# Outputs out of the partner's buffer, a ring of four row tiles, three pairs of weight buffers, slot 4 loaded behind the last store

## The reference

```
g_sel = argmax(x1 @ w_group + b_group)               # 1 of 4 groups
top_i = top_k(e_sel + e_bias, 2)                     # 2 of its 8 experts
for e in range(32):                                  # d_expert = 256
    gu = xt @ w_gate_up[e]                           # 1024 x 512
    h = silu(gu[:, :256]) * gu[:, 256:]
    y = y + gate[:, e:e+1] * (h @ w_down[e])         # 256 x 1024
out = layernorm(ALPHA * x1 + y, ln2_g, ln2_b)
```

## Time and profile before

| | us |
|---|---|
| median of 3 runs | 601.82 (601.57 to 604.54) |
| the profiled execution | 602.56 |
| its span | 600.9 |
| PE busy | 518.8 (86%) |
| DVE busy | 373.2 (62%) |
| ACT busy | 191.4 (32%) |
| POOL busy | 134.0 (22%) |
| chain that ended last | PE 56%, DMA 26%, DVE 8%, ACT 7% |
| queue of SP (weights) | 127.46 MB, 52.9% of the 16 engines' span |
| queue of POOL (rows) | 29.59 MB, 13.0% |

### The profile page before, as it was taken

How to read it: one execution, slowest core, us unless ns; L and a number is a source line. 1 busy time by engine, 2 the same in 40 slices (tenths; PEclk the granted TensorE clock), 3 DMA queues, 4 the chain that set the end, 5 groups by cost and what they waited for, 6 DMA issues and landing times.

```text
span 600.9 us, 8960 instructions
## 1 busy us (share of the span) xinstructions
PE 518.8 (86%) x3296; PEld 281.0 (47%) x3296; DVE 373.2 (62%) x722; ACT 191.4 (32%) x356; POOL 134.0 (22%) x156
## 2 busy tenths in 40 slices
PE   5999999999979879899999898888887777767761
PEld 4887788874355443445556743333332222222220
DVE  1642059898933576652258666677886477666686
ACT  0100374214243644121142122444444244432340
POOL 1001054500025760000000201233323222221231
PEclk9999999999979999999999899999999899999997
DMA  9940008570606932001978599999999999999951
GB/s 302 405 155 6 1 1 331 213 269 1 279 5 230 395 116 87 2 1 59 417 290 342 180 420 406 409 396 419 415 415 411 419 418 419 415 415 418 401 193 43
DMA packets 34010, 157.95 MB, mean 263 GB/s; under 512 B 12680, under 2 KB 12680, under 8 KB 20016
## 3 DMA queue, kind: packets, MB, share of 16 engines
q1 hardware_dynamic: 20592, 127.46, 52.9%
q0 software_dynamic: 10752, 29.59, 13.0%
q10 hardware_dynamic: 2624, 0.34, 0.4%
HBM read 160.12 MB, written 21.23 MB: 302 GB/s over the span
## 4 chain that ended last, share of the span: by engine, by line
PE 56%; DMA 26%; DVE 8%; ACT 7%; issue 3%; SPq 0%; POOL 0%; DVEq 0%; POOLq 0%; ACTq 0%
DMA arena_o<-in_w_gu 19%; PE ps L489 17%; PE ps L748 8%; PE ps L962 8%; PE ps L985 4%; PE ps L651 3%; PE ps L589 2%; PE ps L635 2%; DVE arena_s L1477 2%; PE ps L672 2%; DMA first_rows<-arena_s,known 1%; DMA x_rows<-arena_s 1%; PE ps L555 1%; DMA known<-slot_table 1%; DMA slot_table<-arena_s 1%
## 5 line engine op out<-in xcount | busy, mean ns | idle before, releaser
L962 PE MATMUL ps<-arena_w,arena_s 128*64 128x512 f32 x368 | 109.2, 605 | 24.1 <-DMA arena_w<-in_w_gu 12.3
L489 PE MATMUL ps<-arena_w 128*128 128x260 f32 x416 | 94.5, 388 | 6.7 <-DMA arena_w<-in_w_in 6.2
L489 PEld LDWEIGHTS ps<-arena_w 128*128 128x128 f32 x416 | 79.7, 193 | 21.0 <-DMA arena_w<-in_w_in 6.2
L962 PEld LDWEIGHTS ps<-arena_w,arena_s 128*64 128x64 f32 x368 | 33.2, 139 | 96.9 <-issue 66.4
L985 PE MATMUL ps<-arena_w,cs 128*64 128x512 f32 x184 | 56.1, 615 | 20.8 <-ACT cs L1260 20.8
L748 PE MATMUL ps<-arena_o,arena_s 128*128 128x512 f32 x128 | 58.3, 601 | 1.6 <-DVE arena_s L1601 1.6
L962 PE MATMUL ps<-arena_o,arena_s 128*64 128x512 f32 x112 | 50.2, 595 | 0.0
L1477 DVE STREAM_TRANSPOSE arena_s<-arena_w 128x1024 f32<-128x1024 f32 x36 | 41.8, 1214 | 8.3 <-PE ps L589 8.2
L2150 POOL DMA_INDIRECT first_rows<-arena_s,known x15 | 18.0, 1202 | 113.9 <-ACT arena_s L1267 105.1
L1910 DVE TENSOR_TENSOR arena_s<-arena_s,ps 128x256 f32<-128x256 f32 x16 | 6.7, 421 | 56.5 <-ACT arena_s L1256 56.5
L985 PEld LDWEIGHTS ps<-arena_w,cs 128*64 128x64 f32 x184 | 16.0, 141 | 51.0 <-issue 30.3
(11 more groups left out here) (349 smaller groups left out, 897.3 us busy)
## 6 DMA issues: line engine op xcount, KB each, us to landing
arena_w<-in_w_gu SPq DMA_DIRECT2D x46, 1024.0 KB, 19.9
arena_w<-in_w_dn SPq DMA_DIRECT2D x23, 1024.0 KB, 19.9
arena_o<-in_w_gu SPq DMA_DIRECT2D x14, 1024.0 KB, 23.2
arena_o<-in_w_dn SPq DMA_DIRECT2D x7, 1024.0 KB, 23.8
arena_w<-in_w_in SPq DMA_DIRECT2D x13, 512.0 KB, 14.1
arena_o<-in_w_out SPq DMA_DIRECT2D x1, 4096.0 KB, 13.5
arena_s<-in_w_gu SPq DMA_DIRECT2D x4, 1024.0 KB, 8.1
arena_w<-in_xT SPq DMA_DIRECT2D x4, 520.0 KB, 6.7
```

Of the source, the lines that this page charges most:

```text
L489: last = mm(ps[rows, b + n, 0:HALF], lhs(k), rhs(k)[:, n * HALF:(n + 1) * HALF], start=(k == 0), stop=(k == ks - 1))
L962: last = mm(ps[64 * e:64 * e + 64, 2 + q, :], xgT[:, k, CAP * e:CAP * (e + 1)], gu_w[2 * slots + e][:, k, :], start=(k == 0), stop=(k == K ...
```

## The change

1. **Slot 4.** Its two w_gate_up loads are issued right behind the last store of x1, ahead of the waits for the stores and for the first gather. Its w_down load stays where it was.
2. **Weight buffers.** All three pairs of buffers are used all the way, by the table `BUFFER`: pairs 3 to 15 use buffers 0, 1, 2, 0, 1, 0, 1, 2, 0, 1, 2, 0, 1. The refill for pair n waits for the pair that used its buffer last: 3 for 0, 4 for 1, 5 for 2, 6 for 3, 7 for 4, 8 for 6, 9 for 7, 10 for 5, 11 for 8, 12 for 9, 13 for 10, 14 for 11, 15 for 12.
3. **Rows.** The row tiles are a ring of four. The last operation of `finish(n)` writes the finished row into `yo[n % 2]`, the buffer that held the partner's rows, and the output leaves from there; there are two such buffers. `finish(n-1)` stands in DVE's step n, `root(n-1)` in ACT's. On POOL, step n is now `gather_other(n)` (which also waits for the landing of output n-2), `scatter_own(n)`, `scatter_out(n-1)` (behind the landing of output n-2) and `gather_rows(n+3)`; step 0 is `scatter_own(0)` alone.
4. **Residual.** `lng` is multiplied by ALPHA once, ahead of `residual(0)`. The two operations of `residual` take a minimum and a maximum with large constants in place of the multiplications by ALPHA.
5. **End.** DVE's end is `finish(14)`, `hidden(15)`, `finish(15)`; in the last, the partner's rows are added first and the own part, straight from PSUM, behind them. PE has five 128 x 128 products whose result is not used behind the last gate and up products.
6. `bounds_check` of the row DMAs is a register instead of a constant.

```diff
...
+BUFFER = (0, 1, 2, 0, 1, 0, 1, 2)
+ROW_MAX = 1e6
...
-S_XG = [5120, 6144, 0, D, S_RT] + [S_SLOT + D * n for n in range(3)]
-S_YO = [S_SLOT + 3 * D, 2 * D, S_SLOT + 4 * D]
+S_XG = [5120, 6144, 0, D]
+S_YO = [S_RT, 2 * D]
...
+def pair_buffer(n):
+    return n if n < HEAD else BUFFER[(n - HEAD) % BODY]
+def before_in(n):
+    d = 1
+    while BUFFER[(n - HEAD - d) % BODY] != pair_buffer(n):
+        d += 1
+    return d
...
         def ring(n):
-            return n % BODY
-        def other(it, n):
-            return 2 if isinstance(it, tuple) and n == NPAIR - 1 else n % 2
+            return n % 4
...
             store_x1(4)
+            for half in range(2):
+                gate_up(4, slice(4, 5), half)
             landed(sp, x1_stored, TT)
             landed(sp, gathered[0])
-            for half in range(2):
-                gate_up(4, slice(4, 5), half)
             down(4, slice(4, 5))
             sp.dma_start(lng, lns[0:2].partition_broadcast(P)).then_inc(ln1_landed, 16)
             sp.dma_start(lng2, lns[2:4].partition_broadcast(P)).then_inc(ln1_landed, 16)
-            def refill(q, e, used):
+            def refill(it, n):
+                q, used = pair_buffer(n), nth(it, n, add=1 - before_in(n))
...
                 for half, done in enumerate((gu_half, gu_ps)):
                     sp.wait_ge(done, used)
...
-            refill(0, 6, 1)
-            refill(1, 8, 2)
+                for j in range(2):
+                    down(2 * q + j, slice(e + j, e + j + 1) if isinstance(e, int) else bass.ds(e + j, 1))
+            refill(None, HEAD)
+            refill(None, HEAD + 1)
...
-            with sp.Fori(0, n_rounds * (NE // 4) - 3) as it:
-                refill(0, (it * 4 + 10) % NE, it * 2 + 4)
-                refill(1, (it * 4 + 12) % NE, it * 2 + 5)
-            refill(0, NE - 2, past + (NPAIR - 2))
+            with sp.Fori(0, n_rounds * 2 - 1) as it:
+                for n in range(HEAD + 2, HEAD + 2 + BODY):
+                    refill(it, n)
+            for n in range(HEAD + 2 + BODY, NPAIR):
+                refill((past,), n)
...
                 if not last_pair:
                     turn_tokens(it, n + 1)
+                else:
+                    for _ in range(5):
+                        mm(ps[:, 7, 0:P], ident[:, :], ident[:, :], start=True, stop=True)
...
                     own_out(it, n)
-                    root(it, n - 2)
+                    root(it, n - 1)
...
-            root((past,), NPAIR - 3)
+            root((past,), NPAIR - 2)
             hidden((past,), NPAIR - 1, True)
-            root((past,), NPAIR - 2)
             root((past,), NPAIR - 1)
...
             def residual(it, n):
                 x = xg[ring(n)]
-                stt(x, x, ALPHA, lng[:, 0, :], ALU.mult, ALU.mult).then_inc(residual_step, 1)
+                stt(x, x, ROW_MAX, lng[:, 0, :], ALU.min, ALU.mult).then_inc(residual_step, 1)
                 dve.wait_ge(residual_step, nth(it, n, 1, 2, 1))
-                stt(x, lng[:, 1, :], ALPHA, x, ALU.mult, ALU.add).then_inc(residual_step, 1)
-            def own_part(it, n, last_pair=False):
+                stt(x, x, -ROW_MAX * ROW_MAX, lng[:, 1, :], ALU.max, ALU.add).then_inc(residual_step, 1)
+            def own_part(it, n):
                 x, g = xg[ring(n)], known[:, n // QUAD % 2, 2, n % QUAD:n % QUAD + 1]
                 dve.wait_ge(known_landed, nth(it, n, QUAD, 16, 16))
                 dve.wait_ge(residual_step, nth(it, n, 1, 2, 2))
+                dve.wait_ge(ya_done, nth(it, n, add=1))
+                stt(x, yb[n % 2], g, x, ALU.mult, ALU.add).then_inc(own_added, 1)
+            def finish(it, n, last_pair=False):
+                x = xg[ring(n)]
                 if last_pair:
-                    dve.wait_ge(dn_ps, nth(it, n, add=1))
-                    y = ps[:, 5:7, :]
-                    x = x.rearrange("p (a b) -> p a b", a=2)
+                    dve.wait_ge(residual_step, nth(it, n, 1, 2, 2))
                 else:
-                    dve.wait_ge(ya_done, nth(it, n, add=1))
-                    y = yb[n % 2]
-                stt(x, y, g, x, ALU.mult, ALU.add).then_inc(own_added, 1)
-            def finish(it, n):
-                x = xg[ring(n)]
-                dve.wait_ge(own_added, nth(it, n, add=1))
+                    dve.wait_ge(own_added, nth(it, n, add=1))
                 if n > 0:
-                    dve.wait_ge(yo_landed[other(it, n)], 16 if other(it, n) == 2 else nth(it, n + 1, 2, 16))
-                    stt(x, yo[other(it, n)], known[:, n // QUAD % 2, 3, n % QUAD:n % QUAD + 1], x, ALU.mult, ALU.add).then_inc(finish_step, 1)
+                    dve.wait_ge(yo_landed[n % 2], nth(it, n + 1, 2, 16))
+                    stt(x, yo[n % 2], known[:, n // QUAD % 2, 3, n % QUAD:n % QUAD + 1], x, ALU.mult, ALU.add).then_inc(finish_step, 1)
                     dve.wait_ge(finish_step, nth(it, n, 1, 4, 1))
                     dve.wait_ge(mean_done, nth(it, n))
+                if last_pair:
+                    halves = x.rearrange("p (a b) -> p a b", a=2)
+                    dve.wait_ge(dn_ps, nth(it, n, add=1))
+                    stt(halves, ps[:, 5:7, :], known[:, n // QUAD % 2, 2, n % QUAD:n % QUAD + 1], halves, ALU.mult, ALU.add).then_inc(own_added, 1)
+                    dve.wait_ge(own_added, nth(it, n, add=1))
...
-                stt(x, x, stat[:, 2:3], lng2[:, 1, :], ALU.mult, ALU.add).then_inc(out_ready, 1)
+                stt(yo[n % 2], x, stat[:, 2:3], lng2[:, 1, :], ALU.mult, ALU.add).then_inc(out_ready, 1)
...
-                if n >= 2:
-                    finish(it, n - 2)
+                if n >= 1:
+                    finish(it, n - 1)
                 own_part(it, n)
...
+            link(ts(lng[:, :, :], lng[:, :, :], ALPHA, None, ALU.mult))
...
-            finish((past,), NPAIR - 3)
+            finish((past,), NPAIR - 2)
             hidden((past,), NPAIR - 1)
-            finish((past,), NPAIR - 2)
-            own_part((past,), NPAIR - 1, True)
-            finish((past,), NPAIR - 1)
+            finish((past,), NPAIR - 1, True)
...
             def gather_other(it, n):
...
+                if n >= 2:
+                    pool.wait_ge(out_landed, gone)
                 pool.wait_ge(scattered[(n - 1) % 2], before)
-                G.indirect_dma_start(out=yo[other(it, n)], out_offset=None, in_=first_rows,
+                G.indirect_dma_start(out=yo[n % 2], out_offset=None, in_=first_rows,
                                      in_offset=bass.IndirectOffsetOnAxis(ap=place(1, n), axis=0),
-                                     bounds_check=TOK - 1, oob_is_err=False).then_inc(yo_landed[other(it, n)], 16)
-            def scatter_out(it, n):
-                ready, = number(nth(it, n, add=1))
+                                     bounds_check=limit, oob_is_err=False).then_inc(yo_landed[n % 2], 16)
+            def scatter_out(it, n, ready=None, before=None):
+                if ready is None:
+                    ready, before = number(nth(it, n, add=1), nth(it, n, 1, 16))
                 fixed()
+                if n > 0:
+                    pool.wait_ge(out_landed, before)
                 pool.wait_ge(out_ready, ready)
                 G.indirect_dma_start(out=y_out, out_offset=bass.IndirectOffsetOnAxis(ap=place(1, n), axis=0),
-                                     in_=xg[ring(n)], in_offset=None, bounds_check=TOK - 1,
+                                     in_=yo[n % 2], in_offset=None, bounds_check=limit,
                                      oob_is_err=False).then_inc(out_landed, 16)
             def pair_step(it, n):
-                scatter_own(it, n)
-                if n >= 3:
-                    outs, = number(nth(it, n - 2, 1, 16))
-                    fixed()
-                    pool.wait_ge(out_landed, outs)
-                if n >= 2:
-                    scatter_out(it, n - 2)
                 if n >= 1:
                     gather_other(it, n)
-                if n == 1:
-                    pool.wait_ge(dn_ps, HEAD)
-                if n < HEAD:
-                    gather_rows(n + 4, first_at[:, n + 4:n + 5])
-                elif not isinstance(it, tuple) or n + 4 < NPAIR:
-                    gather_rows(n + 4, rows_at.bitcast(I32)[:, (n + 4) // QUAD % 2, n % QUAD:n % QUAD + 1])
+                scatter_own(it, n)
+                if n >= 1:
+                    scatter_out(it, n - 1)
+                    m = n + 3
+                    if n < HEAD:
+                        gather_rows(m, first_at[:, m:m + 1])
+                    elif not isinstance(it, tuple) or m < NPAIR:
+                        gather_rows(m, rows_at.bitcast(I32)[:, m // QUAD % 2, m % QUAD:m % QUAD + 1])
...
```

More of the change, by code:

```diff
@@ L1312, in _ @@
                 own_out((past,), n)
-                root((past,), n - 2)
+                root((past,), n - 1)
                 if n % QUAD == QUAD - 1:
@@ L2215, in _ @@
                 pair_step((past,), n)
-            n = NPAIR - 1
-            gather_other((past,), n)
```

(9 more changed lines are left out.)

37 lines of the change are left out of this document (21 added, 16 removed).

## The result

The changed kernel takes 608.18 us (median of 8 runs, 607.05 to 611.54), the kernel before 602.47 on the same chip (8 runs). The ratio is 1.0097, interval 1.0076 to 1.0118: slower by 1%, where 597.5 was forecast. The profiled execution has a span of 606.8 (600.9 before).

What follows compares the result with a forecast made beforehand. The weight stream was taken to set the end. The span, 600.9, changes by -4.5 from the stream, +2.4 at hidden(15), -2.1 behind it, to 596.7; forecast time 597.5 us, 8-in-10 range 593.5 to 604.0.

Steps and rivals of the forecast that it cites:

- Slot 4: Two w_gu loads issued at about 329.4 instead of 342.3 fill the stream's hole: gain 5.0 us, 0.3 charged to first gather.
- Three pairs of buffers: Weight refills: 0 by itself, but keeps slot 4's 5.0 us, of which two pairs would give back 3.4 at 389.1.
- The later steps' loop: Row DMAs from gather_other to the next into the same buffer: 24.9 us for two pairs against TensorE's 26.8, so hidden.
- 564.5 plus 9.6 = 574.1: Tail: gather of pair 14's partner rows issued at 564.5, taking 9.6 us, landed at 574.1.
- The delay at pair 6: TensorE 6 us later (bounds 1 and 12.5), under the 7.7 of queued weights left at pair 8's refill: price 0.
- inside the same cover: gather_rows(4), issued at 386.4, lands at 394 to 398 for transposes due at 392.3, hidden by the delay already counted.
- the third rival: TensorE starts too late, from gather_other(1) to finish(1) and pair 8's refill; stream runs dry: some 605 us, chance 0.15.
- share of unknown tail waits: Unnamed waits at the kernel's end, counted with the third rival in the 0.17 chance of a slower kernel.
- So it waits 1.8: Tail, VectorE: finish(14) waits 1.8 us for its partner rows and ends at 580.1.
- +2.4 back at hidden(15): Tail, VectorE: hidden(15), following finish(14), starts 2.1 us earlier, not 4.5, so 2.4 of the stream's gain is lost.
- The 5.0 for the last products: Tail, TensorE: down products of pair 15 take 5.0 us (bounds 3.65 and 5.0), after standing about 3 us.
- the first rival: More gained: clock holds in the last products (-1.35), no 1.8 wait, rows faster as stream ebbs: about 594 us, chance 0.13.

Runs made afterwards that it cites:

- slot4_only: The kernel before with only slot 4's two w_gate_up loads moved ahead of the two waits: 602.31 us against 602.83, ratio 0.9999.
- full_late_slot4: gather_14_first without its step-14 exception, and with slot 4's gate_up loads put back behind the waits: 603.45 us, ratio 1.0011 to the kernel before.
- gather_14_first: own_first_tail with weight buffer table 0,1,2,0,1,2,0,1, and in step 14 alone gather_other(14) ahead of scatter_own(14): 598.52 us, ratio 0.9931 to the kernel before.
- full_2_buffers: own_first_tail with two pairs of weight buffers instead of three: 603.69 us, ratio 1.0010 to the kernel before.
- own_first_tail: The changed kernel with scatter_own ahead of gather_other, and hidden(15) ahead of finish(14) (ScalarE: root(14)): 600.6 us, ratio 0.9962 to the kernel before.
- tail_order: The changed kernel with hidden(15) ahead of finish(14) on VectorE and ahead of root(14) on ScalarE: 604.07 us, ratio 1.0016 to the kernel before.
- free_buffer_15: gather_14_first with pair 15's partner rows gathered into the row buffer pair 12 has left: 598.83 us, ratio 0.9939 to the kernel before.
- tail_late_pairs: tail_order with weight buffer table 0,1,2,0,1,2,0,1 in place of 0,1,2,0,1,0,1,2: 605.29 us, ratio 1.0043 to the kernel before.
- own_first: The changed kernel with scatter_own(n) ahead of gather_other(n) on GpSimd, nothing else: 607.43 us, ratio 1.0075 to the kernel before.
- two_buffers: The changed kernel with only two pairs of weight buffers in the table: 607.13 us, ratio 1.0061 to the kernel before.

## Why the prediction was wrong

**Slot 4** was right. The share in 332 to 340 is 1.01, the loads go at 330.44. slot4_only gives back 3.6 at 384 to 392 (3.4 forecast), and full_late_slot4 against gather_14_first shows 4.9 of the 5.0 (less 0.3). The first gather was charged 0.3. In this execution it lands 1.1 later than before (SP goes on at 343.42, not 342.28), but hidden(2) of slot4_only is at 379.33, as in the kernel before (379.35), so the delay need not be the request's.

**Three pairs of buffers**: "it is what makes the 5.0 real" was right, by full_2_buffers. "By itself 0" was right only for the stream. It left out that the gap which it fills at 384 to 389 was where the row DMAs of pair 1 ran fast.

**The later steps' loop is the step that failed.** The forecast of the span, 596.7, was missed by 10.1, and 10.0 of them stand in one term of its tail: the partner's rows of pair 14, "564.5 plus 9.6 = 574.1", came at 574.88 plus 9.24 = 584.1. The prediction has the loop as "24.9 for two pairs, where TensorE needs 26.8", hidden "until 13.4 a pair". The sum followed one buffer: gather_other, finish, output, next gather_other into the same buffer. But the engine's own queue closes a shorter loop: gather_other(n+1) waits for the landing of output n-1, and scatter_out(n) is queued behind gather_other(n+1). So each output waits for the one before it, though they are in different buffers (scatter_out's own wait for the output before it asks the same), and the loop is passed once a pair: the landing, 0.9 until gather_other is issued (386.25 + 10.4 to 397.51), and 2.6 to 3.8 from there to the next scatter_out, 2.9 at the median. With 8.0 for the landing, the median that I took, that is 11.8 and hidden. With 10.9, as third of a burst, it is 14.7, as measured, and not hidden. So the loop was sized wrong twice: how often it is passed, and a median taken over another order of issue. Exchanging scatter_own and gather_other takes most of the wait away (112.1 us, 18.6 in own_first_tail) and with it the loop in the middle. The rows of before had held the warning: the 9.6 of gather_other against 8.0 of out_y is the third place against the second, and I read it as two kinds of row DMA.

**The delay at pair 6** was mis-sized, and not by the loop. Forecast 6 against a margin of 7.7. hidden(3) is at 397.78, 5.0 later, at the lower end of what I wrote. But TensorE turns the rows of pair 4 ahead of that, and the term for them, landing "between 8.0 and 11.9 later" and so "inside the same cover", was too short: issued at 387.55, they took 12.5, as fourth of a burst, and the transposes came at 400.11. And the term had no price for the clock: behind 6.67 of standing TensorE's next 8 transposes and 16 products ran at 0.50, 2.3 longer. So hidden(4) is 10.2 later. The rows of pair 6, now in the loop (issued at 417.27, 13.5 to land), add 1.5: hidden(6) is at 444.79 (433.04 before), 11.8 later, as is pair 8's refill. The rule "each us beyond 7.7 costs one" gives 4.1 us of dry stream and 6.0 are missing; the other 1.9 I have not broken down.

That is the third rival, with its place (the refill of pair 8) and its sign; I gave it 0.15. Its "605" from a delay of 15 lies near the measured time by luck. By itself the hole only takes back what slot 4 had brought: with the hole left in and the tail's order exchanged the kernel is where it was before (tail_order, 1.0016). The rest is the tail, of which no rival says more than the "share of unknown tail waits".

**The tail.** gather_other(14) was to be issued at 564.5 and comes at 574.88: 383.58 and 13 steps of 14.7 is 10.4 more than the timetable, which let the row DMAs follow the stream's pace without a loop of their own. "So it waits 1.8" is 6.98, and hidden(15), forecast at 580.1, stands at 589.69. tail_order shows its price: 0.8% in the ratios, 4.9 us (6.3 between the profiled spans, 606.8 and 600.5, but tail_order's is among its fastest). That hidden(15) stands behind a DMA wait on VectorE is a danger that I saw ("+2.4 back at hidden(15)") and sized by the timetable alone. The 5.0 for the last products, at a clock that falls again, came near (5.34), though TensorE stood 7.1 ahead of them and not about 3; where it stood for 0.5 us ahead of them (free_buffer_15) they took 3.67, as the first rival had it. The 2.1 gained behind them were right.

**Which of the two is the loss?** Neither alone. With the tail put right the loop still ends last (tail_order, tail_late_pairs); with the loop gone the tail is as late as before (own_first); with both gone the stream decides and slot 4 brings its 5 us. Three limits lay within a few us of each other, each hiding what the removal of another would give.

**Rows behind weights.** The Trainium skill, "DMA: Bandwidth & Descriptors", section "Queues, rings and completion order", says that a DMA engine takes turns between the queues that have work. The traces agree as far as depth goes: in the kernel before, a pair's first weight load takes 10.8 us to land at 402.6 and 25.6 at 456.2, and the first row DMA of the burst beside it 8.7 (401.01) and 8.2 (454.46). They show beside it what the prediction had only in a rival and at the tail, and did not weigh at 384: with the weight queue empty the same DMA takes 3.7.

## What to carry to other kernels

When an order is changed on an engine that issues DMAs, write the waits and the queue positions down as one cycle and ask how often it is passed: two buffers give no second lap when the release of one stands in the queue behind the wait for the other. Take a DMA's time from the rows that have its place in the burst, not from its kind's median. Price a stall of TensorE with what runs behind it: here 6.67 us of standing were followed by 2.3 us of slower products. And put no wait for a transfer ahead of the instruction that feeds the last products.

## What the runs showed of the hardware

A gather or scatter of 128 rows of 4 KB from GpSimd's queue, in a stream of about 415 GB/s, lands in 8.2 to 8.3 us as first of a burst, 8.1 to 9.5 as second, 9.7 to 10.9 as third and 11.9 to 13.3 as fourth; with the stream dry, a gather in 3.7 (two_buffers, 382.66) or 4.2 (the changed kernel, 439.03). I had expected neither the order by place nor, outside the tail, the fast rows of a dry stream. The time depends on whether weights flow, hardly on how many are queued (8.7 and 8.2 beside loads that take 10.8 and 25.6).

TensorE's granted clock fell from 1.00 to 0.50 while TensorE stood 6.67 us for rows and was 0.50 from 398 to 406; the sixteen down products begun there took 5.10, and 3.65 where the clock was 1.00.
